# RWKV inversion on 32x32 quads inside 64-step chunks, and side products three column chunks at a time

## The reference

```
def step(state, inp):
    r_t, w_t, k_t, v_t, a_t, b_t = inp
    sa = jnp.einsum('bhvk,bhk->bhv', state, a_t)
    state = (state * w_t[:, :, None, :] + sa[..., None] * b_t[:, :, None, :]
             + v_t[..., None] * k_t[:, :, None, :])
    return state, jnp.einsum('bhvk,bhk->bhv', state, r_t)
xs = (rh, wh, kh, vh, -kk, kk * ah)
```

## Time and profile before

| | us |
|---|---|
| time, median of 3 (2665.2 to 2670.97) | 2666.25 |
| the profiled execution's own time | 2674.42 |
| its span | 2672.6 |
| PE busy in the span | 2451.4 (92%) |
| DVE busy | 1412.8 (53%) |
| ACT busy | 747.2 (28%) |
| mean granted TensorE clock | 0.965 of full |

### The profile page before, as it was taken

The page is one execution under the profiler, slowest core; times in us unless marked ns, Lnnn a source line. Parts: engine busy times, 40 slices in busy tenths (PEclk is TensorE's granted clock), DMA queues, the critical chain, the costliest instruction groups (busy, mean ns, idle before and its releaser), DMA issues. The chain is left out here.

```text
span 2672.6 us, 45804 instructions
## 1 busy us (share of the span) xinstructions
PE 2451.4 (92%) x18445; PEld 1837.2 (69%) x18445; DVE 1412.8 (53%) x3009; ACT 747.2 (28%) x1365; POOL 63.8 (2%) x101
## 2 busy tenths in 40 slices
PE   6999999868989898996988889899999999999998
PEld 4566888636646566663655657788888888888886
DVE  3357888825537455432655555755533533533443
ACT  3226888033224142211544542122100100100101
POOL 0020000000000000000111100000000000000000
PEclk8989999979989999997999999999999999999999
DMA  6432232252222212224868846311111111111112
GB/s 176 118 102 82 66 98 66 74 169 68 58 82 58 74 53 73 53 71 126 280 208 268 272 133 227 115 48 32 48 32 48 33 47 48 32 48 33 47 32 75
DMA packets 289104, 252.05 MB, mean 94 GB/s; under 512 B 53575, under 2 KB 240553, under 8 KB 288766
## 3 DMA queue, kind: packets, MB, share of 16 engines
q1 hardware_dynamic: 211382, 198.95, 23.9%
q10 hardware_dynamic: 77512, 50.18, 6.8%
HBM read 200.49 MB, written 48.59 MB: 93 GB/s over the span
## 5 line engine op out<-in xcount | busy, mean ns | idle before, releaser
L1205 PE MATMUL rwkv_banks<-h_chunk,w_gate 128*128 128x384 f32 (+1 forms) x768 | 286.7, 506 | 29.2 <-DMA w_gate<-in_w_in 21.6
L2815 DVE TENSOR_TENSOR x<-x,ps_mm 128x272 f32<-128x272 f32 x280 | 120.9, 435 | 308.1 <-PE ps_mm L2782 308.0
L2806 ACT COPY merged_then_hidden<-ps_mm 128x272 f32<-128x272 f32 x160 | 61.7, 386 | 719.9 <-PE ps_mm L2782 719.9
L2782 PE MATMUL ps_mm<-merged_then_hidden,w_mm 128*128 128x272 f32 x960 | 227.1, 393 | 1.6 <-DVE sums_of_right_sides_ L3035 0.9
L1205 PEld LDWEIGHTS rwkv_banks<-h_chunk,w_gate 128*128 128x128 f32 x768 | 142.5, 200 | 106.5 <-issue 27.8
L2782 PEld LDWEIGHTS ps_mm<-merged_then_hidden,w_mm 128*128 128x128 f32 x960 | 182.2, 190 | 39.9 <-DVE sums_of_right_sides_ L3035 1.3
L2782 PE MATMUL ps_mm<-v_T_and_gates_then_h_mlp,w_mm 128*128 128x272 f32 x864 | 204.5, 392 | 0.0
L2782 PEld LDWEIGHTS ps_mm<-v_T_and_gates_then_h_mlp,w_mm 128*128 128x128 f32 x864 | 164.1, 190 | 33.9
L2782 PE MATMUL ps_mm<-sums_of_right_sides_,w_sums_mm 128*128 128x272 f32 x704 | 165.3, 392 | 0.5 <-DVE sums_of_right_sides_ L2993 0.5
L2815 DVE TENSOR_TENSOR merged_then_hidden<-merged_then_hidden,ps_mm 128x272 f32<-128x272 f32 x120 | 51.4, 434 | 195.4 <-PE ps_mm L2782 195.4
L557 PE MATMUL first_banks<-hT,w_pr 128*128 128x384 f32 (+3 forms) x432 | 150.3, 507 | 3.8 <-PEq L188 3.8
(11 more groups left out here) (483 smaller groups left out, 4199.7 us busy)
## 6 DMA issues: line engine op xcount, KB each, us to landing
k_pages<-in_cache_k SPq DMA_DIRECT2D x128, 256.0 KB, 3.4
v_pages<-in_cache_v SPq DMA_DIRECT2D x128, 256.0 KB, 5.3
w_gate<-in_w_in ACTq DMA_DIRECT2D x48, 512.0 KB, 4.2
w_mm<-in_w_mlp_in SPq DMA_DIRECT2D x32, 512.0 KB, 4.8
w_mm<-in_w_mlp_out SPq DMA_DIRECT2D x32, 512.0 KB, 4.9
w_pr<-in_w_in SPq DMA_DIRECT2D x27, 512.0 KB, 5.3
v_T_and_gates_then_h_mlp<-gates_T SPq DMA_DIRECT2D x16, 544.0 KB, 4.7
gates_T<-gate_rows ACTq DMA_DIRECT2D x32, 192.0 KB, 4.2
```

The source lines that it names most:

```text
L1205: ins = MM(B[:, GB, 0:w], gw[:, n % 2, k_, :], hc[:, k_, 0:w], start=(k_ == 0), stop=(k_ == KO - 1))
L2782: ins = self.nc.tensor.matmul(self.ps[:, c, self.BANK[step], 0:272], left[step][:, k, :], right[step][:, k, 272 * c:272 * c + 272], start= ...
L2806: self.nc.scalar.copy(self.target(step, rows, c), self.out(act, u, step, c)).then_inc(self.by_act, 1)
L2815: self.nc.vector.tensor_tensor(to, to, ps, ALU.add).then_inc(self.by_dve, 1)
```

## The change

1. **Quads.** X and XT are kept as 32x32 diagonal blocks: `xx` is [128, 2, 2, 8, 32], and a product over a half is `by_quad`, 32 matmuls 32x32x32 on the four diagonal 32x32 tile positions, into half a bank. `turned_products` goes; in its place `unfold` fetches the diagonal quads and their transposes with two `by_quad`s against an identity. The series and two levels run on quads. The third level (32 to 64) is done once, off the diagonal: `last_p` and `last_x`, 16 matmuls each a half; ScalarE then puts the four quadrants together into a new tile `xw` with 12 copies a round of 32 partitions, after 4 copies of `last_p`'s result. `invert` reads `xw`.
2. **Banks.** A half of the inversion uses one bank (`IB` = 7, 5) where it used two; `products` alternate between two pairs of banks (`AB` = 2, 4, 2, 4), and g = 3 no longer waits for the evacuation of g = 2.
3. **Side products.** The three chunks of one side product go back to back into three banks (`FB`, `WXB`, `EB`; others at the two ends of the stage), after the round's products are evacuated.
4. **Order.** New times: `raw_k` is loaded first and the first prelude's key part starts first; side products stand between the hops and none in the samples; the bonus moves from the samples into the round; gate slots are moved (hops 5 a step, levels 6, last step 2, samples up to 6); 58 gate matmuls are left for the end where 36 were.

```
-SERIES, LV = 3, 3
+SERIES, LV = 3, 2
...
-    AB, IB, ORB, SA = (2, 4, 2, 2), (4, 2), (6, 7), (3, 5)
+    AB, IB, SA = (2, 4, 2, 4), (7, 5), (3, 5)
...
+    WHOLE = {"pe_za": (1, 2, 3), "pe_zb": (4, 5, 6), "pe_ss": (7, 1, 2), "gn_mean": (FB, YB, EB), "gn_var": (FB, YB, EB),
+             "pe_g": (SB, WXB, 5), "pe_bon": ()}
...
+    def beside(made, i):
+        alone = i == 0 and made in ("pe_za", "pe_zb", "pe_ss") or i == HP - 1 and made in ("gn_mean", "gn_var", "pe_g")
+        return WHOLE[made] if alone else (FB, WXB, EB)
...
-    T = 116.0
-    SERIES_AT, LEVEL, GROUP, SAMPLE = 7.0, 25.0, 50.0, 86.0
+    T = 118.0
+    SERIES_AT, LEVEL, LAST, GROUP, SAMPLE = 6.0, 30.0, 46.0, 52.0, 88.0
...
+            def side(i, in_round, made, kept, left, right):
+                if 0 <= in_round < HP:
+                    pe.wait_ge(S["a_kept"], in_round * 8 + 8)
+                for b, (t0, w) in zip(beside(made, i), CH):
+                    clear(b)
+                    times[kept] = times.get(kept, 0) + 1
+                    emptied[b] = (S[kept], times[kept])
+                    MM(B[:, b, 0:w], left, right(t0, w), start=True, stop=True).then_inc(S[made], 1)
...
-                if g == 3:
-                    pe.wait_ge(S["a_kept"], i * 8 + 6)
...
-            def by_chunk(bank, left, right):
+            def by_quad(bank, o, left, right, quads=range(4)):
                 for n in range(8):
-                    for e in range(2):
-                        ins = MM(B[HS[e], bank, n * 64:n * 64 + 64], left[HS[e], n, :], right[HS[e], n, :], start=True,
-                                 stop=True)
+                    for q in quads:
+                        ins = MM(B[Q[q], bank, o + n * 32:o + n * 32 + 32], left(n, q), right(n, q), start=True, stop=True)
                 return ins
...
             def level_x(i, L, l):
                 pe.wait_ge(S["p_kept"], i * 2 * LV + 2 * l + L + 1)
-                if l < LV - 1:
-                    by_chunk(IB[L], xt[:, L, :, :], pm[:, L, :, :])
-                by_chunk(IB[L] + 1, pm[:, L, :, :], xt[:, L, :, :]).then_inc(S["x_made"], 1)
+                by_quad(IB[L], 0, of(xt, L), of(pm, L), range(0, 4, 1 if l < LV - 1 else 2))
+                by_quad(IB[L], 256, of(pm, L), of(xt, L)).then_inc(S["x_made"], 1)
...
+            def last_x(i, L):
+                pe.wait_ge(S["xw_kept"], i * 16 + 2 * L + 2)
+                for n in range(8):
+                    for e in range(2):
+                        ins = MM(B[Q[2 * e], IB[L], n * 32:n * 32 + 32], pm[Q[2 * e + 1], L, n, :],
+                                 xt[Q[2 * e + 1], L, n, :], start=True, stop=True)
+                ins.then_inc(S["x_made"], 1)
...
+            def assemble(i, L):
+                for q in range(4):
+                    nc.scalar.copy(xw[Q[q], 8 * L:8 * L + 8, 32 * (q % 2):32 * (q % 2) + 32], xt[Q[q], L, :, :])\
+                        .then_inc(S["xw_kept"], 1)
+                act.wait_ge(S["x_made"], i * (2 * LV + 2) + 2 * LV + L + 1)
+                for e in range(2):
+                    nc.scalar.copy(xw[Q[2 * e], 8 * L:8 * L + 8, 32:64],
+                                   B[Q[2 * e], IB[L], 0:256].rearrange("p (n c) -> p n c", n=8))\
+                        .then_inc(S["xw_kept"], 1)
```

More of the change, by code:

```diff
@@ L1170, in _ @@
             sp.dma_start(w2a2[64:128, :], a["rwkv_a2"]).then_inc(S["lora_in"], 16)
-            load(0, "raw_k")
             for half in range(2):
@@ L1207, in gates @@
                         ins.then_inc(S["gate_made"], 1)
[L1209 to L1220 removed]
+            emptied = {}
@@ L1235, in prelude, with key_norms @@
+            def key_norms():
+                for i in range(HP):
+                    yield prelude_at(i, 24.0, 6.0)
                     pe.wait_ge(S["act_sq"], i + 1)
-                    for c_ in side("pe_ss", "act_ss", p.halves[:, :], square):
-                        yield prelude_at(i, 30.0 + 3 * c_)
+                    side(i, i - 1, "pe_ss", "act_ss", p.halves[:, :], lambda t0, w: kn[:, t0:t0 + w])
             def bonuses():
                 for i in range(HP):
-                    rk = lambda t0, w: bons[i % 2][:, t0:t0 + w]
@@ new lines, in of, with diagonal, unfold @@
+            def of(t, L):
+                return lambda n, q: t[Q[q], L, n, :]
+            def diagonal(L):
+                return lambda n, q: aa[Q[q], 8 * L + n, 0, 32 * (q % 2):32 * (q % 2) + 32]
+            def unfold(i, L):
+                pe.wait_ge(S["a_kept"], i * 8 + 4 * L + 4)
+                if i and L == 0:
+                    pe.wait_ge(S["y1_kept"], i * 2)
+                eye = lambda n, q: const("eye32")[Q[q], :]
+                by_quad(IB[L], 0, diagonal(L), eye)
+                by_quad(IB[L], 256, eye, diagonal(L)).then_inc(S["p_made"], 1)
@@ L1541, in rounds @@
                             level_x(i, L, l)
+                    for L in range(2):
+                        yield T * i + LAST + L
+                        last_p(i, L)
+                    yield T * i + LAST + 1.2
+                    weigh_values(i, 1)
+                    for L in range(2):
+                        yield T * i + LAST + 3.0 + L
+                        last_x(i, L)
                     for g in range(4):
@@ L1575, in rounds @@
                                 .then_inc(S["so_made"], 1)
-            weave(rounds(), normalise(), prelude(), bonuses(), gates())
+            weave(rounds(), normalise(), decays(), key_norms(), bonuses(), gates())
         @block.scalar
@@ new lines, in decays @@
+                    for c_, (t0, w) in enumerate(CH):
+                        yield prelude_at(i, 17.5 + 0.7 * c_, 4.0 + 0.7 * c_)
+                        if i and c_ == 0:
+                            act.wait_ge(S["tilde"], i)
+                        act.wait_ge(S["pe_za"], i * 3 + c_ + 1)
+                        nc.scalar.activation(lw[:, t0:t0 + w], B[:, beside("pe_za", i)[c_], 0:w], ACT.Sigmoid,
+                                             bias=vec[:, i, 0:1]).then_inc(S["act_za"], 1)
@@ L1765, in _ @@
             load_gate(1)
-            act.wait_ge(S["pool"], 1)
-            weave(rounds(), normalise(), prelude(), gates())
+            act.wait_ge(S["pool"], 2)
+            weave(rounds(), normalise(), decays(), keys(), gates())
             for b in range(2):
```

390 lines of the change are left out of this document (190 added, 200 removed).

## The result

The changed kernel takes **2633.47 us** (median of 4, 2630.77 to 2633.88) where the kernel before, beside it on the same chip, takes 2668.61: ratio 0.9849, 95% interval 0.9823 to 0.9875. It is 35 us faster, 1.5%. The time lies in the forecast's range (2560 to 2665) and on its side, but 43 us above the 2590 forecast: half of the gain came. By a mark of 2% the two kernels would count as the same, for which the forecast left a chance of 0.03. From here on, `L` numbers are lines of the kernel that the sentence speaks of; in the changed one L1303 is `by_quad`, L1351 `last_p`, L1359 `last_x`, L1217 the gates, L1236 the side products.

The account below looks back on a forecast made before the run. TensorE's own queue was taken to set the RWKV stage's length. Inversion -50, side products -18, products -10, clock -7, start -10, end -6 and additions +26 sum to -75 us: 2590 us from a median of 2666.25, range 2560 to 2665.

Parts of the forecast that it names:

- Inversion, -50: Inversion on four tile positions at 8 ns a record: 18 instead of 31 us a round, -50 us in the stage.
- My slow rival: Issue binds at 25 ns a record: the inversion gives +60 us instead of -50, 2686 us in all; chance 0.17.
- Side products -18: In the rounds, side chunks no longer wait for their own product's evacuation, thanks to three banks: -18 us.
- products -10: The fourth group of products no longer waits for DVE to empty the third, four times: -10 us.
- added +26: New waits in the last cross step, levels and samples, together +26 us, bounds 8 and 50.
- (a): Last cross step: PE waits for ACT's new copies and DVE's additions, 3.5 us a round, +14 us.
- (b): Levels: PE gets faster while DVE's queue keeps reciprocal, scan and norms between masks and sums, 2 us a round, +8.
- (c): Samples: no bonus chunk covers the wait for `sample_G`, and a gate matmul before the transposes is gone: +4 us.
- Clock -7: The low clock after the fourth group's wait goes, 1.7 us lost each of four times: -7 us.
- Start -10: Start of the stage: `raw_k` loaded first lets DVE start earlier, and waits for the single bank go: -10 us.
- Helpers bind: ACT's copies and DVE's queue hold each level and the last cross step, +42 us, 2632 us; chance 0.13.
- 16 ns a record: Inversion records no faster than the fastest row shows: -4 us instead of -50, 2630 us in all; chance 0.2.

Follow-up runs that it names:

- both good edits: Changed kernel with the unfold's identity product as 4 matmuls of 256 columns and more gate matmuls in levels and last cross step: 2594.64 us, ratio 0.9712.
- gates in the hops: On top of both good edits, each hop gets 6 instead of 5 gate matmuls, each group's second slot 1 instead of 2: 2611.72 us, ratio 0.9750.
- the doubled copies: Changed kernel with four more ACT copies of 32x256 elements a half in the last cross step, into a spare tile: 2634.75 us, ratio 0.9869.

## Why the prediction was right and wrong

- **Faster, and TensorE's queue as the bound: right.** Taking stops from PE moved the whole by as much or more (12, 19 and 39 us), work added to ACT did not. That the time fell in the range is in part luck: terms that were wrong by tens of us stood against each other.
- **Inversion, -50: the step that failed.** The pace in a burst was right (9 ns a record; 16 to 17 on two positions), and by the ledger the inversion's work fell from 29.5 to 20.6 us a round, -36 where -50 was reckoned. Of the missing 14 some 6 are the kernel before, where I had put 31 us a round, and the rest is mostly the switches between kinds of matmul: 64 records take 0.68 us from the first start to a gate matmul's (642.26 to 642.94), 0.58 to the next product's (18 such switches in the first round), so the mean over all is 11 ns a record. The larger error was the sentence "nothing by issue". I looked at what starts a record once it is there, and asked 32 records for it; 3712 instructions a round, 256 of them in some 3.7 us, I did not look at. This is +27 us. My slow rival had this in its last clause ("after which the queue may run dry"), with a constant 25 ns a record as the price; the truth is 9 ns in store and 29 ns beyond it, so the other work between the quads decides. The floor of about 25 ns between starts, which the prediction quotes from the Trainium skill ("TensorE: Matmul & The Clock Gate", Part 1, "Wait — 56ns, not 53.3ns?"), does not hold over four positions, as 605.50 to 606.72 shows: 128 records in 1.22 us.
- **Side products -18, products -10, added +26: wrong in the parts, the waits better in sum.** The idle time at waits in the rounds fell by 22, where -18 - 10 + 26 makes -2. The side waits went as forecast. Of the additions (a) and (b) hardly exist here: twice as many copies cost 2 us, within the spread, and L1351 waits 0.4 us for DVE. In the levels PE was held by its own supply, which covered the helpers; with the gate loads left out the wait of L1351 for DVE is 2.4 us, and with both good edits and gates in the hops `invert` waits 5.2. In the groups and samples PE does wait more: 4.5 us more at L1385 for ACT, which I had not reckoned, and 4.2 at L1511 for DVE, where (c) had +4. Of the products' wait 8.5 us went from the list, but 5.6 of them put back cost nothing that can be told.
- **Clock -7: wrong in sign.** The rounds lose 22 to 32 us to the low clock, 18.8 before. The low stretches behind the products' waits did go, but others came: in the first profile five of the ten stretches at 1.2 GHz in the rounds, 34 us (17 lost), begin in or within 3 us after a stop. With 13 us of stops the loss was 13.7, with 38 it was 37.5; with 29 and the extra waits of two products in one bank 42.7. In between the order is rough, and the size of one term is open, as two looks at one kernel differ by 10.
- **Start -10: right in size (-11.8), in its reason wrong in part.** The load's place, undone, costs nothing. The six side waits are gone (4.7 us) and the wait for `b_tilde` too (3.7), PE's waits for its gate units' evacuation grew by 1.7, and the clock lost 2.6 us there instead of 6.5, which I had not reckoned.
- **End -6:** the tail grew by 5.7 with 24 gate matmuls more, some 15 us of work at 0.32 us a record, so about -9 beside them: about right.
- Sum for the rounds: +27 (supply), +14 (pace), +10 to +21 (clock against -7), -20 (waits) makes 31 to 42 us. Forecast were -76 in the rounds with the 22 gate matmuls that leave them (17 us); the two profiles show -36 and -42.
- **Rivals.** Helpers bind: out for the changed kernel, by the doubled copies; they begin to once the supply is better. 16 ns a record: the time is near (2630), the mechanism is not. Side waits only move: out, as undoing two of them costs 22 us. That the banks made most of the gain stays open.

## What to carry to other kernels

When work is cut into many small matmuls, count instructions, not only array time: here TensorE got 256 instructions in 3.5 to 3.75 us, 5.5 beside a large load, with hardly more than one block in store. Before reading an idle stretch without a releaser as this, see that it stands at a multiple of 256 instructions. Spread long matmuls among the short ones so that each 256 instructions last that long, and merge products that share weights into one wide matmul; the two together were worth 39 us here, more than the change itself. Price an idle stretch of TensorE above its length, since the lower clock may follow, and put no exact figure on the clock from one profile.

## What the runs showed of the hardware

- PE's instruction supply as above: stops at multiples of 256 instructions, 16 KB packets that take about 1.1 us, a block every 3.5 to 3.75 us with quiet DMA (all: 2.6 to 4.0), 5.5 with a 512 KB load beside it and 6.9 once.
- 32x32 tiles on four positions: 64 records in 0.53 to 0.58 us, each weight load 104 ns, which is 31 less than the 135 of 64 columns.
- A matmul of 32x32 weights by 256 columns on four positions costs what eight of 32 columns cost (0.57 us for the four), with an eighth of the instructions.
- Twelve waits of 13.2 us together made a kernel 22 us slower; 5.6 us of waits at the groups of products made it no slower.
